# A reordered head loop in a two-layer attention and expert kernel, with part of the softmax scaling moved to GpSimd

## The reference

```
mod = silu(cvec) @ w_ada + b_ada                  # six rows of 1024: sh1 sc1 g1 sh2 sc2 g2
u = rmsnorm(h, norm1_g) * (1 + sc1) + sh1
q, k, v, a_glu, gates = split(u @ w_in)
q, k = rope(rmsnorm(q)), rope(rmsnorm(k))         # context tokens: no rope
s = (q . k) / 8                                   # 16 heads of 64, 4 key heads
p = softmax(s)                                    # latent: over 128 cached + 512 own keys
attn_br = (p @ v) @ w_attn_o                      # context: over its own 128 keys
conv_br = silu(layernorm(conv31(glu(a_glu)))) @ w_conv_o
h = h + g1 * ((sigmoid(ga) * attn_br + sigmoid(gc) * conv_br) @ w_out)
h = h + g2 * experts(u2)                          # 16 experts, two per token
```

## Time and profile before

| | us |
|---|---|
| median of 3 runs | 2059.42 |
| lowest and highest | 2053.09 to 2059.61 |
| the profiled execution | 2066.88 |
| its span | 2065.3 |
| TensorE busy | 1623.8 (79%) |
| VectorE busy | 1319.0 (64%) |
| ScalarE busy | 798.7 (39%) |
| GpSimd busy | 603.3 (29%) |

### The profile page before, as it was taken

One profiled execution on the slowest core, in us unless ns is written; L12 is line 12 of the kernel. 1 busy time (PEld: TensorE's weight loads), 2 busy tenths in 40 slices (PEclk: granted clock), 3 DMA queues, 4 the chain that ended last, 5 costly groups with the idle time before them and its releaser, 6 DMA issues.

```text
span 2065.3 us, 28036 instructions
## 1 busy us (share of the span) xinstructions
PE 1623.8 (79%) x8938; PEld 1382.6 (67%) x8938; DVE 1319.0 (64%) x2022; ACT 798.7 (39%) x1250; POOL 603.3 (29%) x282
## 2 busy tenths in 40 slices
PE   2699588878998894899649968777799969579880
PEld 0589455568998784777538955556799968567760
DVE  0656578789882636587284838778889262648734
ACT  0412456563123222566231336556312231346631
POOL 2122100013442210498411310001333331048751
PEclk8799789988999895899869979998899989689995
DMA  8412134411222334699762204441122225459985
GB/s 292 152 45 78 47 128 159 143 42 32 62 70 64 144 142 182 226 363 363 288 212 67 62 27 162 136 153 49 45 62 62 62 83 214 163 178 355 365 313 214
DMA packets 131211, 310.11 MB, mean 150 GB/s; under 512 B 11636, under 2 KB 81396, under 8 KB 109984
## 3 DMA queue, kind: packets, MB, share of 16 engines
q1 hardware_dynamic: 104096, 224.41, 32.0%
q0 software_dynamic: 16400, 42.90, 5.6%
q10 hardware_dynamic: 10560, 40.90, 5.2%
HBM read 287.06 MB, written 39.44 MB: 158 GB/s over the span
## 4 chain that ended last, share of the span: by engine, by line
PE 48%; issue 16%; DVE 14%; DMA 11%; POOL 5%; ACT 5%; DVEq 1%; ACTq 0%; POOLq 0%; SPq 0%
PE ps L527 13%; PE ps L486 8%; PE ps L740 6%; PE ps L591 4%; POOL w_lo L2131 4%; PE ps L445 2%; DVE probs L1592 2%; PE ps L571 2%; PE ps L786 2%; DVE gu_lo L1404 2%; DMA raw_x<-in_w_down 2%; DMA raw<-in_w_down 2%; PE ps L573 1%; PE ps L600 1%; PE ps L806 1%
## 5 line engine op out<-in xcount | busy, mean ns | idle before, releaser
L2131 POOL TENSOR_TENSOR w_lo<-raw,w_hi 128x2048 fp32r<-128x2048 f32 (+1 forms) x60 | 259.3, 4329 | 547.1 <-ACT w_hi L1047 547.1
L527 PE MATMUL ps<-u_hi,w_hi 128*128 128x320 f32 x768 | 243.7, 317 | 29.8 <-POOL w_lo L2131 29.4
L527 PE MATMUL ps<-u_hi,w_lo 128*128 128x320 f32 x768 | 242.1, 315 | 0.0
L527 PE MATMUL ps<-u_lo,w_hi 128*128 128x320 f32 x768 | 241.9, 315 | 0.0
L1704 DVE SCALAR_TENSOR_TENSOR cv<-glu,convw,cv 128x670 f32<-128x670 f32 x240 | 236.0, 1059 | 0.0
L1047 ACT ACTIVATE w_hi<-raw 128x2048 fp32r<-128x2048 f32 (+1 forms) x64 | 101.4, 1592 | 317.4 <-PE ps L527 151.2
L527 PEld LDWEIGHTS ps<-u_hi,w_hi 128*128 128x128 f32 x768 | 148.7, 194 | 32.9 <-issue 32.9
L1608 DVE TENSOR_TENSOR pt_lo<-ps,pt_hi 128x512 fp32r<-128x512 f32 x160 | 108.7, 690 | 69.9 <-ACT pt_hi L1168 68.1
L527 PEld LDWEIGHTS ps<-u_lo,w_hi 128*128 128x128 f32 x768 | 148.5, 193 | 0.1
L527 PEld LDWEIGHTS ps<-u_hi,w_lo 128*128 128x128 f32 x768 | 148.3, 193 | 0.0
L1168 ACT ACTIVATE pt_hi<-ps 128x512 fp32r<-128x512 f32 x160 | 93.5, 597 | 139.3 <-PE ps L591 138.0
(11 more groups left out here) (367 smaller groups left out, 4272.8 us busy)
## 6 DMA issues: line engine op xcount, KB each, us to landing
raw<-in_w_ada SPq DMA_DIRECT2D x52, 1024.0 KB, 6.4
raw<-in_w_in SPq DMA_DIRECT2D x48, 512.0 KB
raw_x<-in_w_gate SPq DMA_DIRECT2D x16, 1024.0 KB, 7.1
raw<-in_w_up SPq DMA_DIRECT2D x16, 1024.0 KB
raw_x<-in_w_down SPq DMA_DIRECT2D x16, 1024.0 KB, 9.7
raw_x<-in_w_up SPq DMA_DIRECT2D x14, 1024.0 KB, 8.7
raw<-in_w_gate SPq DMA_DIRECT2D x14, 1024.0 KB
raw<-in_w_down SPq DMA_DIRECT2D x14, 1024.0 KB
```

What stands on the lines that cost most here:

```text
L527: ins = mm(ps[:, b, 0:HALF], (w_hi, w_lo)[w][:, s, cols(k):cols(k) + P], xs[x][:, k, half * HALF:(half + 1) * HALF], start=(k == 0 and w + ...
L2131: g_.tensor_tensor(w_lo[:, n % 2, 0:k], raw[:, n % 2, 0:k], w_hi[:, n % 2, 0:k].bitcast(F32), ALU.subtract).then_inc(*G.up("g_lo", "w_lo", n))
```

## The change

The head loop is written in another order on all three engines. TensorE makes two score tiles of the next head before the transposes of the present one, and each of the other two between them. ScalarE takes exponentials and high halves in turn; VectorE does likewise with maxima and low halves. There are two query buffers (`q_sts`), filled one pair of heads ahead behind transposes 3 of every even head; query and probability transposes share banks 4 and 5 in turn, and the context output uses bank 3. VectorE's `inverse` keeps the reciprocal, and `normalise` (four scalings a head) moves to GpSimd, which also stores the modulation rows at heads 5 and 9 and behind head 15. VectorE makes the low halves of the first two gate units behind its last `output`. At the start the n1col matmul moves behind piece 3, and the five copies behind the broadcast of the modulation rows. One of two waits before an expert's matmuls goes (the other implies it).

```diff
-    q_st = at("q_st", [P, 2, NTOK], F32R, R_A + 36 * KB)
+    q_sts = [at("q_st0", [P, 2, NTOK], F32R, R_A + 36 * KB), at("q_st1", [P, 2, NTOK], F32R, R_W + 12 * KB)]
-        eng.wait_ge(*T.at("n1_in"))
-        b = fill(("n1T",))
-        mm(ps[0:DEPTH * KC, b, 0:P], n1col[:, :, :].rearrange("p l k -> p (l k)"), ident[:, :], start=True, stop=True).then_inc(*T.filled(("n1T",)))
         for k in range(KC):
             ada("first", k, raw_slot(k % 4), T.at("w_first", k))
+            if k == 3:
+                eng.wait_ge(*T.at("n1_in"))
+                b = fill(("n1T",))
+                mm(...)
# TensorE, q_transposes and p_transposes
-                b = fill(("qT", h2, 0), 2)
+                b = fill(("qT", h2, 0), 4 + next(turn) % 2)
-                b = fill(("PT", h, kc), 4 + (h * NT + kc) % 2)
+                b = fill(("PT", h, kc), 4 + next(turn) % 2)
-                b = fill(("Oc", h), 0)
+                b = fill(("Oc", h), 3)
# TensorE, head loop
             for h in range(NH):
-                if h + 1 < NH and (h + 1) % 2 == 0:
-                    q_transposes((h + 1) // 2)
+                scores(h + 1, 0)
+                scores(h + 1, 1)
                 eng.wait_ge(*T.at("probs", h))
                 p_transposes(h, 0)
                 p_transposes(h, 1)
+                scores(h + 1, 2)
+                values(h, 0)
+                p_transposes(h, 2)
+                if h < ADA_HEADS:
+                    ada_of(2 * h)
+                scores(h + 1, 3)
+                values(h, 1)
+                p_transposes(h, 3)
                 if h:
                     ctx_values(h - 1)
-                (ada, scores, transposes and values in the old order)
+                if h % 2 == 0 and h + 2 < NH:
+                    q_transposes(h // 2 + 1)
                 if h < ADA_HEADS:
                     ada_of(2 * h + 1)
+                ctx_scores(h + 1)
+                values(h, 2)
                 p_transposes(h, 4)
                 ctx_transpose(h)
                 values(h, 3)
                 values(h, 4)
# ScalarE, head loop
             for h in range(NH):
-                if h + 1 < NH and (h + 1) % 2 == 0:
-                    q_hi((h + 1) // 2)
+                exps(h + 1, 0)
                 probs_hi(h, 0)
+                exps(h + 1, 1)
                 probs_hi(h, 1)
+                exps(h + 1, 2)
+                probs_hi(h, 2)
+                exps(h + 1, 3)
+                probs_hi(h, 3)
                 if h:
                     ctx_out_half(h - 1)
+                if h % 2 == 0 and h + 2 < NH:
+                    q_hi(h // 2 + 1)
+                ctx_exp(h + 1)
                 probs_hi(h, 4)
                 ctx_hi(h)
                 out_half(h)
# VectorE
-            def normalise(h, tiles):
+            def inverse(h, tiles):
-                v.reciprocal(rsum[:, h % 2, t0:t1], rsum[:, h % 2, t0:t1]).then_inc(*V.step())
-                eng.wait_ge(*V.at("v", V.steps))
-                for t in tiles:
-                    ins = v.tensor_scalar(probs[:, h % 2, t, :], probs[:, h % 2, t, :], rsum[:, h % 2, t:t + 1], None, ALU.mult)
-                    ins.then_inc(*V.up("v_p", *(("probs", h) if t == LT - 1 else ())))
+                v.reciprocal(rsum[:, h % 2, t0:t1], rsum[:, h % 2, t0:t1]).then_inc(*V.up("v_rs", "rsum", h, t1 - 1))
             for h in range(NH):
+                maxima(h + 1, 0)
+                maxima(h + 1, 1)
                 probs_lo(h, 0)
                 probs_lo(h, 1)
                 if h in (4, 8, 12):
                     modulation(MOD_ORDER[h // 4 - 1])
                 if h == 12:
                     scale_row(0)
+                maxima(h + 1, 2)
+                inverse(h + 1, range(0, 2))
+                probs_lo(h, 2)
+                maxima(h + 1, 3)
+                probs_lo(h, 3)
                 if h:
                     ctx_output(h - 1)
+                if h % 2 == 0 and h + 2 < NH:
+                    q_lo(h // 2 + 1)
+                inverse(h + 1, range(2, LT))
+                ctx_maximum(h + 1)
                 probs_lo(h, 4)
                 ctx_normalise(h + 1)
                 ctx_lo(h)
                 output(h)
+            lo(U_GATE)
+            lo(U_GATE + 1)
             ctx_output(NH - 1)
# GpSimd, before the layers
-        for t in range(NT):
-            dma(h_d[t * P:(t + 1) * P, :], io["x_all"][t * P:(t + 1) * P, :], "h_st")
         modulated_rows()
+        for t in range(NT):
+            dma(h_d[t * P:(t + 1) * P, :], io["x_all"][t * P:(t + 1) * P, :], "h_st")
# GpSimd, in a layer
-            modulation(1)
-            bias(0, DEPTH - 1 - l)
-            modulation(2)
+            def normalise(h, tiles):
+                eng.wait_ge(*G.at("rsum", h, tiles[-1]))
+                eng.sem_inc(sems("passed_G"), 1)
+                for t in tiles:
+                    ins = g_.tensor_scalar(probs[:, h % 2, t, :], probs[:, h % 2, t, :], rsum[:, h % 2, t:t + 1], None, ALU.mult)
+                    ins.then_inc(*G.up("g_p", *(("probs", h) if t == LT - 1 else ())))
+            for h in range(NH):
+                normalise(h, range(0, 2))
+                normalise(h, range(2, LT))
+                if h == 5:
+                    modulation(1)
+                    bias(0, DEPTH - 1 - l)
+                if h == 9:
+                    modulation(2)
             modulation(0)
-            for n in range(U_GATE, U_GATE + 2):
-                lo(n)
```

More of the change, by code:

```diff
@@ L17 @@
+import itertools
 from contextlib import ExitStack
@@ L458, in _ @@
             ada("first", k, raw_slot(k % 4), T.at("w_first", k))
+            if k == 3:
+                eng.wait_ge(*T.at("n1_in"))
+                b = fill(("n1T",))
+                mm(ps[0:DEPTH * KC, b, 0:P], n1col[:, :, :].rearrange("p l k -> p (l k)"), ident[:, :], start=True, stop=True).then_inc(*T.filled(("n1T",)))
         for name, by in (("ov_yfull", 1), ("ov_gu", 1), ("ov_xt", 1)):
@@ L549, in _ @@
             eng.wait_ge(*T.at("q_ready"))
+            turn = itertools.count()
             def q_transposes(h2):
-                b = fill(("qT", h2, 0), 2)
+                b = fill(("qT", h2, 0), 4 + next(turn) % 2)
                 for t in range(LT):
@@ L557, in q_transposes @@
                 ins.then_inc(*T.filled(("qT", h2, 0)))
-                b = fill(("qT", h2, 1), 3)
+                b = fill(("qT", h2, 1), 4 + next(turn) % 2)
                 ins = nc.tensor.transpose(ps[:, b, 0:P], q_tok[:, LT, h2 * P:(h2 + 1) * P], ident[:, :])
@@ L1131, in q_hi @@
                     for x in range(2):
-                        if h2 >= 1 and part == 0:
-                            eng.wait_ge(*A.at("filled", ("Sc", 2 * h2 - 2 + x)))
-                        act(q_st[0:DH, x, c0:c0 + n], ps[x * DH:(x + 1) * DH, b, 0:n], ACT.Copy, scale=DH ** -0.5).then_inc(*A.up("a_q", "q_hi", h2, part, x))
+                        if h2 >= 2 and part == 0:
+                            eng.wait_ge(*A.at("filled", ("Sc", 2 * h2 - 4 + x)))
+                        act(q_sts[h2 % 2][0:DH, x, c0:c0 + n], ps[x * DH:(x + 1) * DH, b, 0:n], ACT.Copy, scale=DH ** -0.5).then_inc(*A.up("a_q", "q_hi", h2, part, x))
             def exps(h, t):
@@ L1401, in lo @@
                         eng.wait_ge(*V.at("mod_out", "first"))
-                    v.tensor_tensor(w_of(n, 0), raw[:, n % 2, :], w_of(n, 1).bitcast(F32), ALU.subtract).then_inc(*V.up("v_lo", "w_lo", n))
+                    if n == U_GATE:
+                        eng.wait_ge(*V.at("arow", 0))
+                    if n == U_GATE + 1:
+                        eng.wait_ge(*V.at("mod_out", 2))
+                        eng.wait_ge(*V.at("mod_out", 0))
+                    k = size(n)
+                    v.tensor_tensor(w_of(n, 0)[:, 0:k], raw[:, n % 2, 0:k], w_of(n, 1)[:, 0:k].bitcast(F32), ALU.subtract).then_inc(*V.up("v_lo", "w_lo", n))
                     return
@@ L1559, in q_lo @@
                     for x in range(2):
-                        ins = v.scalar_tensor_tensor(out=q_st[DH:P, x, c0:c0 + n], in0=ps[x * DH:(x + 1) * DH, b, 0:n], scalar=DH ** -0.5,
-                                                     in1=q_st[0:DH, x, c0:c0 + n].bitcast(F32), op0=ALU.mult, op1=ALU.subtract)
+                        ins = v.scalar_tensor_tensor(out=q_sts[h2 % 2][DH:P, x, c0:c0 + n], in0=ps[x * DH:(x + 1) * DH, b, 0:n], scalar=DH ** -0.5,
+                                                     in1=q_sts[h2 % 2][0:DH, x, c0:c0 + n].bitcast(F32), op0=ALU.mult, op1=ALU.subtract)
                         if x == 1:
@@ L1634, in _ @@
             ctx_maximum(0)
-            normalise(0, range(LT))
+            inverse(0, range(0, 2))
+            inverse(0, range(2, LT))
             ctx_normalise(0)
             for h in range(NH):
-                if h + 1 < NH and (h + 1) % 2 == 0:
-                    q_lo((h + 1) // 2)
+                maxima(h + 1, 0)
+                maxima(h + 1, 1)
                 probs_lo(h, 0)
@@ L2020, in _ @@
```

(4 more changed lines are left out.)

46 lines of the change are left out of this document (5 added, 41 removed).

## The result

The changed kernel takes 2154.77 us (median of 4 runs, 2153.86 to 2157.81), the kernel before 2059.52 beside it: ratio 1.0466, 95% interval 1.0433 to 1.0499. It is 95 us slower; forecast were 2138, in a range of 2112 to 2175. The profiled execution has a span of 2156.3 us against 2065.3 (2156.25 and 2065.35).

What follows compares the result with a forecast made beforehand. Attention's head loop was taken as bound by VectorE's work plus TensorE holes, afterwards by VectorE and ScalarE queues waiting on each other. Two layers +86.7, attention's end +6.8, start -15: +78.5 us, median 2138, range 2112 to 2175.

Steps and rivals of the forecast that it cites:

- The ring: Head loop: VectorE and ScalarE queues wait on each other in a closed cycle, making a turn 15.48 us; chance 0.86.
- GpSimd's scaling: Head loop: row scaling on GpSimd takes 0.75 us a tile (bounds 0.59 to 3.9), hidden up to 2.5 us each.
- query halves: Head loop: high and low halves of the query add 2.4 us in 7 of 15 turns, 16.8 in all.
- half-clock cost: Head loop: after holes TensorE runs at 1.2 GHz, last value matmuls 0.45 us later a turn, 6.8 a layer.
- the 2.4 of the modulation: Head loop: three modulation additions and one row scaling, 0.6 us each, add 2.4 us over the fifteen turns.
- alternating banks: Head loop: banks 4 and 5 in turn take away waits that don't end last; no time counted.
- The start: Kernel start: w_ada pieces used as they land, first work earlier; -15 us, with ends -10 and -19.
- The end: End of attention: VectorE halving the first two gate units delays the gate matmuls 3.4 us a layer, 6.8 in all.
- VectorE's relief: Rival, head loop: scaling taken off VectorE shortens a turn to 12.3 us, giving 1990 us; chance 0.05.
- TensorE at 1.2 GHz throughout: Rival, head loop: TensorE at half clock bounds the 12 turns with ada work, giving 2195 us; chance 0.05.
- GpSimd blocked for 3.9 us a tile: Rival, head loop: scaling blocked beside VectorE costs 2.7 us a turn, +81, giving 2219 us; chance 0.02.
- No change (the second rival): Rival, head loop: shorter handovers give a turn of 14.6 us, nothing measurable, time 2059 us; chance 0.02.

Runs made afterwards that it cites:

- a_max_earlier: Changed kernel with VectorE's maximum 2 moved ahead of low half 1 and maximum 3 ahead of low half 2: 2119.1 us, ratio 1.0293 to the kernel before.
- b_half_scale: Changed kernel with GpSimd scaling only the first 320 of each tile's 640 columns, the rest left unscaled: 2152.1 us, ratio 1.0459 to the kernel before.
- c_scale_dve: Changed kernel with the row scaling put back on VectorE, in the new order: 2177.0 us, ratio 1.0567 to the kernel before.
- c_ada_only: Changed kernel with only TensorE's first ada piece of a turn moved behind the transposes of block 3: 2155.7 us, ratio 1.0454 to the kernel before.
- d_start_n1: Kernel before with the change's start alone, plus the n1col load issued right behind the first load: 2048.8 us, ratio 0.9931 to the kernel before.
- e_gate_pool: Changed kernel with the low halves of the first two gate units put back on GpSimd: 2150.7 us, ratio 1.0418 to the kernel before.
- d_start_only: Kernel before with the change's start alone (n1col transpose and x_all copies moved later): 2053.5 us, ratio 0.9957 to the kernel before.
- f_scale_pool: Kernel before, in its own queue orders, with the row scaling alone moved to GpSimd: 2252.8 us, ratio 1.0926 to the kernel before.

## Why the prediction was right

**The ring**, the step that decided the sign, held in sign and size: 4.45, 3.13, 3.13 and 4.77 against 4.36, 3.09, 3.08 and 4.71 us. Loop and its start together were put at +43.4 a layer and measured +46.7 and +48.1. a_max_earlier shows the cause by opening it; b_half_scale and c_scale_dve show that GpSimd's scaling does not stand in its place, and c_ada_only the same for the ada piece.

**Two terms in it were off and nearly cancelled.** That the loop's total fits this well (+42.7 and +45.2 against +42.2) is in part luck. I count a turn from its first pt_lo to that of the next, in layer 1. The six turns without query halves and gate conversions took 15.26 or 15.27 us four times, 15.64 and 15.75 once each: 92.4 together, where six of 15.93 are 95.6. They needed little of the half-clock cost (0.45 each): the granted clock is 1.00 from 327.45 to 342.69. The seven turns with query halves took 18.25 to 20.03, together 133.7, where seven of 18.33 and the 2.4 of the modulation are 130.7. The one of head 6 took 19.13 from max 0 to max 0 (342.69 to 361.82), 3.9 more than the turn before it and not 2.4. There TensorE's last query transpose waits for pt_lo 3, because both use the same one of the banks 4 and 5, and behind this hole its clock falls:

```profile
353.38 0.48 PE L563 MATMUL ps<-ident,q_tok 128*128 128x128 f32 x1 [2.43 <-DVE pt_lo L1611]
```

```profile
353.38:359.73 6.35, 5.84 (x21) 2.94 (x21) 3.42 (x9) 2.41 (x8) 3.20 (x2) 0.53 0.44 151
```

At granted 0.53 the ada piece takes 1.93 us, PT 4 comes late, and ScalarE waits 0.97 for it. It is the pattern of the earlier trace rows, where 6.2 us at 0.50 followed a hole. The wait of 2.43 us stands in all seven of these turns. The forecast had said of the alternating banks only that they take waits away; here they add one. No run changed the banks alone.

**GpSimd's scaling** was the worst-sized term: 0.75 us taken, 1.88 measured, above the 1.62 that I had bounded by the subtraction. It cost next to nothing in the turns, where 2.5 us each were hidden (b_half_scale: 1.3 and 0.5 us a loop), and 3.9 and 2.9 us at the loop's start in layers 1 and 2, where four stand in series, against 1.2 in the forecast (from the projection to the first transposes it is 169.4 us with the scaling on VectorE, in c_scale_dve, and 174.6 in after). The Trainium skill (GPSIMD Engine Reference, Engine selection) has one-input elementwise operations there as "roughly line-rate". VectorE took 551 ns for the same instruction, and 1883 ns is no such rate.

**The start** failed in the step that took n1col to land as before. Its load, the last that GpSimd issues, now lands at 33.1, with the four further pieces in flight beside it. It gave 8.6 and not 15, the largest error of a single term (+6.4). d_start_n1, where n1col goes ahead, gains 13.6 and so shows that the late landing is the cause; how much of the delay is the pieces' and how much that of GpSimd's own loads was not separated.

**The end** was put at 3.4 a layer and is 4.3 and 5.5. VectorE's two subtractions take 3.43 us, as forecast, and TensorE waits 3.64 and 3.65 us for the first of them. The rest lies in the last head, which I had called unchanged: the last value matmul (of the context tile) starts 9.64 and 10.83 us behind its first transposes, against 9.11 and 9.13 before. In e_gate_pool, without the subtractions on VectorE, it is 9.79 and 9.68, and the gates follow at once. The stretches behind the gates came out 5.1 us shorter, which I had put at nothing. In d_start_only, which has the old waits at the experts, the longest of them (layer 1, output projection to the next layer) takes 349.1 us, as in after; so the halved wait does not explain it, and the differences between runs of one code are as large.

**The whole.** The sum missed the span by 12.4 us: 6.4 at the start, 8.1 in the two loops with their starts, 3.0 at the ends, less the 5.1 behind the gates. The median came out 17 above the forecast, because I had also taken off the 7.5 us by which the profiled execution lay above the median; of the changed kernel it lies 3.0 above.

**The rivals.** VectorE's relief does not win (of its 113.4 us idle in the loop it waits 99.5 for pt_hi); TensorE at 1.2 GHz throughout is refuted by the mean of 0.87; GpSimd blocked for 3.9 us a tile by 1.88. No change (the second rival) is out with +4.7%. In the old order, as f_scale_pool shows, GpSimd's plain 1.88 us a tile costs 191 us: there the slow scaling is not hidden, and no blocking is needed for a loss.

## What to carry to other kernels

Write the two queues of engines that hand work to each other side by side and follow one wait through both: where each next operation of one stands behind an operation that needs the other, the turn is the sum of their latencies, whatever their busy times are. Move work to a slower engine only where it can start early enough to be covered, and look at what a small load will be queued behind once the large ones are no longer held back. When a ring is opened, work out the next bound (here the serial end of a turn, then TensorE's clock and its own stretch) before promising the whole gain.

## What the runs showed of the hardware

- GpSimd's row scaling of 128x640 takes 1.88 us and of 128x320 1.08 us; VectorE's 0.55.
- VectorE's context scaling (128x128 in SBUF) takes 671 ns on the mean in after's first loop, 287 where GpSimd does no scaling (c_scale_dve) and 288 where its half-size scalings have nearly ended by then (b_half_scale). The Trainium skill (SBUF — State Buffer, Who interferes with whom) describes an exclusive lock between the two for such operations, under which the loser fully blocks. At 495.36 VectorE's instruction took 0.71 while GpSimd's pair of scalings ran from 493.34 to 497.08: it was slowed by 0.4 and not held to GpSimd's end, so the trace agrees with the contention and not with its length.
- A small load that GpSimd issued at 11.2 us behind eight others, with the DMA moving 414 GB/s (window 4 to 20 us of after), took 21.8 us to land; in before, with 404 GB/s in the same window and no further pieces behind it, 11.1; issued second, at 2.34 (d_start_n1), 6.1.
- In e_gate_pool GpSimd's two gate subtractions take 6.87 us under the last head (4.55 of it for 2048 numbers); its next one, beside VectorE's convolution, takes 12.45 for 2048 numbers, as in the earlier trace rows.
